# A third weight piece ahead, norms in place, and the query sums moved ahead of the rotations in a two-block fp32 transformer kernel

## The reference

```python
# block 1, per layer (L = 16 + 512)
h = rms_norm(x, norm_g)
z = h @ w_in
q = rms_norm(aq per head, q_norm_g);  k = rms_norm(ak per head, k_norm_g)
q = apply_partial_rope(q, cos, sin);  k = apply_partial_rope(k, cos, sin)
ya = sliding_window_sink_attention(q, k, v, sink) * silu(ag)     # 16 heads of 64, 2 kv heads
mq, mk = silu(causal_depthwise_conv(mq | mk))
log_i = mi + b_i;  log_f = log_sigmoid(mf + b_f)                  # the gates' logs
hm = rms_norm(mlstm_chunkwise(mq, mk, mv, log_i, log_f))
y = concat(ya, hm * sigmoid(mo) * silu(mgate)) @ w_out
x = x + y
```

## Time and profile before

| | |
|---|---|
| median of 3 runs | 3089.79 us (3086.59 to 3089.86) |
| the profiled execution | 3090.76 us, its span 3088.9 us |
| PE busy | 2958.4 us, 96% of the span |
| DVE, ACT, POOL busy | 1617.1, 1264.7, 181.9 us |
| mean granted clock of PE | 0.981 |
| DMA | 250.24 MB, mean 81 GB/s |
| block 1, layers 0 and 1 | about 25 to 637 and 637 to 1236 us |
| block 2, layers 0 and 1 | about 1264 to 2157 and 2186 to 3089 us |

### The profile page before, as it was taken

How to read it: one execution, slowest core, us unless ns; L and a number is a source line. 1 busy time by engine, 2 the same in 40 slices (tenths; PEclk the granted TensorE clock), 3 DMA queues, 4 the chain that set the end, 5 groups by cost and what they waited for, 6 DMA issues and landing times.

```text
span 3088.9 us, 44910 instructions
## 1 busy us (share of the span) xinstructions
PE 2958.4 (96%) x18366; PEld 2582.2 (84%) x18366; DVE 1617.1 (52%) x3255; ACT 1264.7 (41%) x2640; POOL 181.9 (6%) x207
## 2 busy tenths in 40 slices
PE   8899999988999999999999999999999999999998
PEld 6799888987999889888888877887888888877886
DVE  5666645346675453677433564334677433554324
ACT  4455423244554232565424433223566334433222
POOL 2100000010000000100000000000100000000000
PEclk9899999998999999999999999999999999999999
DMA  3111321211113222322233222333322232222222
GB/s 102 55 44 58 105 67 62 86 48 44 57 57 105 67 80 85 113 86 68 82 110 96 69 82 69 96 96 96 113 87 68 82 117 89 81 70 76 95 96 82
DMA packets 99735, 250.24 MB, mean 81 GB/s; under 512 B 8597, under 2 KB 44845, under 8 KB 99274
## 3 DMA queue, kind: packets, MB, share of 16 engines
q1 hardware_dynamic: 99530, 247.37, 25.2%
HBM read 239.60 MB, written 6.50 MB: 80 GB/s over the span
## 4 chain that ended last, share of the span: by engine, by line
PE 81%; DVE 11%; ACT 4%; issue 1%; DMA 1%; POOL 1%; DVEq 0%; POOLq 0%; SPq 0%; ACTq 0%
PE ps L92 78%; PE ps L95 3%; ACT Z L98 2%; DVE cl L101 2%; DVE Z L101 2%; DVE Z L109 1%; DVE ZR L101 1%; DVE Z L119 1%; DMA st<-in_stream_dram 1%; DVE Z L105 1%; DVE stat L122 1%; ACT ch L98 1%; ACT L98 0%; POOL stat L101 0%; DVE sq L109 0%
## 5 line engine op out<-in xcount | busy, mean ns | idle before, releaser
L92 PE MATMUL ps<-hh,ch 128*128 128x264 f32 (+1 forms) x2688 | 824.6, 348 | 54.2 <-DVE cl L101 32.1
L92 PE MATMUL ps<-hl,ch 128*128 128x264 f32 (+1 forms) x2880 | 851.7, 340 | 0.0
L92 PE MATMUL ps<-hh,cl 128*128 128x264 f32 (+1 forms) x2688 | 811.7, 343 | 0.0
L101 DVE TENSOR_TENSOR cl<-st,ch 128x1024 fp32r<-128x1024 f32 (+1 forms) x436 | 495.8, 1152 | 531.3 <-ACT ch L98 531.1
L92 PEld LDWEIGHTS ps<-hh,ch 128*128 128x128 f32 x2688 | 468.4, 192 | 128.7 <-issue 27.4
L98 ACT ACTIVATE ch<-st 128x1024 fp32r<-128x1024 f32 (+1 forms) x436 | 424.8, 990 | 357.0 <-PE ps L92 328.3
L92 PEld LDWEIGHTS ps<-hl,ch 128*128 128x128 f32 x2880 | 500.1, 192 | 59.1
L92 PEld LDWEIGHTS ps<-hh,cl 128*128 128x128 f32 x2688 | 468.4, 191 | 58.9
L98 ACT ACTIVATE Z<-ps 128x512 f32<-128x512 f32 (+7 forms) x510 | 218.9, 438 | 600.3 <-PE ps L92 479.8
L92 PE MATMUL ps<-ZR,ch 128*128 128x264 f32 (+2 forms) x1728 | 426.5, 342 | 5.6 <-DVE cl L101 5.2
L92 PEld LDWEIGHTS ps<-ZR,ch 128*128 128x128 f32 x1728 | 289.1, 191 | 48.8 <-issue 12.9
(11 more groups left out here) (133 smaller groups left out, 3213.6 us busy)
## 6 DMA issues: line engine op xcount, KB each, us to landing
st<-in_stream_dram SPq DMA_DIRECT2D x372, 512.0 KB, 3.6
st<-in_stream_dram SPq DMA_DIRECT2D x64, 256.0 KB, 3.3
Z<-decay_rows SPq DMA_DIRECT2D x8, 904.0 KB, 6.4
Z<-bias_lines SPq DMA_DIRECT2D x16, 448.0 KB, 4.1
ya_spill<-Z SPq DMA_DIRECT2D x8, 512.0 KB, 4.5
Z<-ya_spill SPq DMA_DIRECT2D x2, 2048.0 KB, 7.7
Z<-in_x_dram SPq DMA_DIRECT2D x4, 512.0 KB, 5.6
Z<-in_mem_dram SPq DMA_DIRECT2D x2, 1024.0 KB, 6.1
```

Of the source, the lines that this page charges most:

```text
L92: return Ins(self, self.e and self.e.matmul(o, a, b, start=start, stop=stop, skip_group_check=True))
L101: return Ins(self, self.e and self.e.tensor_tensor(o, a, b, op))
```

## The change

Five things are changed together.

1. One more `weights()` in the lead-in, so that three pieces instead of two stand converted ahead of PE.
2. The norm writes its result `hn` into the memory that `hl` has, and the subtraction hl = hn − hh is made in place by a step `nrml` of its own, one k later. The two `sq` buffers take no part in it.
3. Query tiles 0 and 1 are projected from `RH`/`RL`. DVE multiplies `rstd` in when it reads them, ACT squares the result and then scales it. The norm's parts 5 to 7 come behind tile 0.
4. `chain()` sorts its steps by stage, so that the odd tile's `qsum` comes ahead of the even tile's `rope`, and a `rope` ahead of a `ropeq`.
5. `gra` and the first two `grf` come ahead of attention, beside the first value projections; the other `grf` are two steps earlier, and so is `grt`.

```diff
@@ norms
     def norms(self, nid, *ks):
         for k in ks:
-            self.put("nrm", nid, k, self.nsq())
+            self.put("nrm", nid, k)
+            if k:
+                self.put("nrml", nid, k - 1)
+            if k == 7:
+                self.put("nrml", nid, 7)
@@ chain, qk
-            for t, n, x in todo:
+            for t, n, x in sorted(todo, key=lambda y: y[2]):
...
-            self.proj(("q", l, t), nid, L, u, t % 2)
+            if t < 2:
+                self.projr(("q", l, t), nid, u, t)
+            else:
+                self.proj(("q", l, t), nid, L, u, t % 2)
@@ block1
-        self.norms(nid, 3, 4)
+        self.norms(nid, 3)
         put("gr", l)
-        self.norms(nid, 5, 6, 7)
...
+        self.norms(nid, 4)
         qk(0, u)
+        self.norms(nid, 5, 6, 7)
...
             fill(a - 3)
+            if a == 0:
+                put("gra", l)
+            else:
+                put("grf", l, a - 1)
             chain()
         for s in range(35):
             if s < 32:
                 put("sA", l, s)
-            if s == 0:
-                put("gra", l)
-            if 1 <= s < 9:
-                put("grf", l, s - 1)
-            if s == 5:
+            if 1 <= s < 7:
+                put("grf", l, s + 1)
+            if s == 3:
                 put("grt", l)
@@ lead-in
-        if k in (4, 6):
+        if k in (4, 6, 8):
             m.weights()
@@ ACT, qkev
-                if t == 8:
-                    act.wait_ge(("kz", l))
-                    act.activation(RS[i], QF[i], ACT.Square).then_inc("act_qk", ("qks", l, t))
+                if t in (8, 0, 1):
+                    act.wait_ge(("qz", l, t), ("tk",))
+                    m = act.activation(RS[i], QF[i], ACT.Square)
+                    if t < 8:
+                        m = act.activation(QF[i], QF[i], ACT.Identity, scale=P(f"qg8_{l}"))
+                    m.then_inc("act_qk", ("qks", l, t))
                     return
@@ DVE, nrm and nrml
-                dve.wait_ge(("rstd", nid), *sqw(n))
-                dve.scalar_tensor_tensor(sq[n % 2][:, 0:T], xT[:, k, L - T:L], g, rstd[:, 0:T], ALU.mult,
+                dve.wait_ge(("rstd", nid))
+                if nid:
+                    dve.wait_ge(("full", ("o1", nid - 1, 7) if nid < 3 else ("o2", 0, 7)))
+                dve.scalar_tensor_tensor(hnf[:, k, 0:T], xT[:, k, L - T:L], g, rstd[:, 0:T], ALU.mult,
                                          ALU.mult).then_inc("dve_ns", ("ns", nid, k))
+
+            def nrml(nid, k):
                 if k % 2 == 0:
+                    T = L if nid < 2 else 512
                     dve.wait_ge(("hh", nid, k))
-                    dve.tensor_tensor(hl[:, k, 0:T], sq[n % 2][:, 0:T], hh[:, k, 0:T].bitcast(F32),
-                                      ALU.subtract).then_inc("dve_hl", ("hl", nid, k), ("sqfree", n))
+                    dve.tensor_tensor(hl[:, k, 0:T], hnf[:, k, 0:T], hh[:, k, 0:T].bitcast(F32), ALU.subtract).then_inc(
+                        "dve_hl", ("hl", nid, k))
```

More of the change, by code:

```diff
@@ L362, in norm @@
         for k in range(8):
-            self.put("nrm", nid, k, self.nsq())
+            self.norms(nid, k)
             if k < 7:
@@ L832, in k8 @@
             return ap.rearrange("p (k t) -> p k t", k=8)
-        xT, hh, hl = k8(sb("xT", 8 * L)[:, :]), k8(sb("hh", 8 * L, F32R)[:, :]), k8(sb("hl", 8 * L, F32R)[:, :])
+        xT, hh = k8(sb("xT", 8 * L)[:, :]), k8(sb("hh", 8 * L, F32R)[:, :])
+        with nc.sbuf_tensor("hn", [128, 8 * L], F32) as HN:
+            pass
+        hnf, hl = k8(HN[:, :]), k8(sb("hl", 8 * L, F32R)[:, :])
         ifh, ifl = sb("ifh", 128, F32R), sb("ifl", 128, F32R)
@@ L954, in program @@
         RL = [[zr(o, 528) for o in (11000, 11528, 12056, 12584, 14784, 15312, 15840, 23712)],
-              [zr(o, 528) for o in (0, 528, 1056, 5952, 6480, 8080, 8608, 9136)]]
+              [zr(o, 528) for o in (1056, 1584, 5952, 6480, 8080, 8608, 9136, 23712)]]
         def windows(ap):
@@ L1538, in nrm0, with nrm @@
                 act.activation(rstd[:, 0:T], rstd[:, 0:T], ACT.Exp, scale=-0.5).then_inc("act_norm", ("rstd", nid))
-            def nrm(nid, k, n):
+            def nrm(nid, k):
                 T = L if nid < 2 else 512
                 act.wait_ge(("ns", nid, k))
-                if nid:
-                    act.wait_ge(("full", ("o1", nid - 1, 7) if nid < 3 else ("o2", 0, 7)))
-                act.activation(hh[:, k, 0:T], sq[n % 2][:, 0:T], ACT.Copy).then_inc("act_hh", ("hh", nid, k))
+                act.activation(hh[:, k, 0:T], hnf[:, k, 0:T], ACT.Copy).then_inc("act_hh", ("hh", nid, k))
             def prep():
@@ L1957, in qkev @@
             def qkev(l, t):
-                if t == 8:
-                    key = ("q", l, 8)
+                if t in (8, 0, 1):
+                    key = ("q", l, t)
                     dve.wait_ge(("full", key), ("rstd", l), *bars(("b1", l)))
-                    dve.tensor_tensor(v2(QF[2]), tok(key, L), v2(rstd[:, :]), ALU.mult).then_inc(
-                        "dve_kz", ("free", key), ("kz", l))
+                    dve.tensor_tensor(v2(QF[t % 3]), tok(key, L), v2(rstd[:, :]), ALU.mult).then_inc(
+                        "dve_qz", ("free", key), ("qz", l, t))
             def vev(l, g):
@@ L2543, in final @@
                                              ALU.mult).then_inc("dve_out", ("fo", a))
-            do = dict(w=w, load=load, xt=xt, raw=raw, qkev=qkev, vev=vev, gr=gr, nrm=nrm, prep=prep, rope=rope, qsum=qsum, ropeq=ropeq, qkn=qkn, swap=swap, vtr=vtr, conv=conv, agev=agev,
+            do = dict(w=w, load=load, xt=xt, raw=raw, qkev=qkev, vev=vev, gr=gr, nrm=nrm, nrml=nrml, prep=prep, rope=rope, qsum=qsum, ropeq=ropeq, qkn=qkn, swap=swap, vtr=vtr, conv=conv, agev=agev,
                       m_s=m_s, m_t=m_t, m_o=m_o, sA=sA, sB=sB, grf=grf, grt=grt, ss0=ss0, mA=mA, mB=mB, hsc=hsc,
@@ L2565, in nrm @@
                     pool.wait_ge(("hh", nid, k))
-                    pool.tensor_tensor(hl[:, k, 0:T], sq[n % 2][:, 0:T], hh[:, k, 0:T].bitcast(F32), ALU.subtract).then_inc(
-                        "pool_hl", ("hl", nid, k), ("sqfree", n))
+                    pool.tensor_tensor(hl[:, k, 0:T], hnf[:, k, 0:T], hh[:, k, 0:T].bitcast(F32), ALU.subtract).then_inc(
+                        "pool_hl", ("hl", nid, k))
             def load():
@@ L2587, in mvones @@
             def mvones(l):
-                pool.wait_ge(*bars(("b1", l)), ("full", ("gr", l)))
+                pool.wait_ge(*bars(("b1", l)), ("full", ("q", l, 1)))
                 pool.memset(MV[:, :, :, 256:258], 1.0).then_inc("pool_ones", ("mvones", l))
@@ L2634, in final @@
                 rsqrt(so[:, 8:12], 1024, ("so2",))
-            do = dict(sqa=sqa, dqkev=dqkev, dex=dex, hsc=hsc, memprep=memprep, dnorm=dnorm, final=final, nrm=nrm, load=load, rope=rope, qsum=qsum, vtr=vtr, mvones=mvones, pn=pn, bar=pool.bar)
+            do = dict(sqa=sqa, dqkev=dqkev, dex=dex, hsc=hsc, memprep=memprep, dnorm=dnorm, final=final, nrml=nrml, load=load, rope=rope, qsum=qsum, vtr=vtr, mvones=mvones, pn=pn, bar=pool.bar)
             for kind, *a in steps:
```

5 lines of the change are left out of this document (2 added, 3 removed).

## The result

The changed kernel takes 3167.39 us (median of 4 runs, 3162.19 to 3168.09) beside 3089.82 of before in the same session (3086.59 to 3091.3): a ratio of 1.0257, 95% interval 1.0244 to 1.027. It is 77.6 us slower. The forecast was 3088 us with a range of 3062 to 3104, so the time lies far outside. The profiled execution has a span of 3165.4 us.

The account below looks back on a forecast made before the run. PE is busy nearly throughout, so only about 130 us idle and lowered-clock time could be saved. Terms −5.4 − 11 − 2.4 − 1 + 5.2 + 0 − 4.4 + 17.2 = −1.8 from 3090.8 gave 3089.0, median 3088; range 3062 to 3104.

Parts of the forecast that it names:

- Held conversions: Conversions waiting for the projection in front to end delay ACT's and DVE's work behind them in block 2: +5.2 us.
- two such places in each layer of block 2: PE's 1.43 us wait for ACT and 3.07 us wait for a DVE copy, lengthened by 1.6 and 1.0 us.
- The bound that I gave: Slow end for the held conversions at block 2's two places: 2 × 2 × 2.1 = +8.6 us.
- The rival on held conversions: Block 1 attention's 15 conversion pairs a layer delay softmax work: +16 us, 3104 (3097 to 3112); chance 0.22.
- The rest of the third piece: Fewer `cl` waits: output projection −5.4, kv and first block 2 projection −11, wait at 1528.93 −2.4, small waits −1 us.
- Sums ahead of rotations: DVE waits for POOL at tiles 4 and 6, delaying `QL` and heads 16 and 24: 4 × 4.3 = +17.2 us.
- POOL and DVE block each other: Rival: the norm's sixteen POOL subtractions beside DVE stretch by 0.55 us each, +8.8, 3097 (3090 to 3100); chance 0.08.
- Norm in place and raw tiles: PE's waits for `hl` vanish, but about 6.6 us of waiting returns at the first value tiles: 0 us net.
- Gates' logs: Table loads leave the first heads' exponentials, so the convolved projection starts earlier: −2.2 us a layer, −4.4 in all.
- The clock: PE's clock falls to half behind long gaps; +2 us charged at query tile 2 and for each rotation pair.
- signs "if right": `cl` waits under 30 us, `hl` waits 0, kv waits nearly gone, gap near 4.7 us ahead of heads 16 and 24.
- signs "wrong": No longer gap at heads 16 and 24, many 1 to 2 us gaps in block 1's attention, or value tiles' piece in time.

Follow-up runs that it names:

- e3: The changed kernel with the chain of steps unsorted, sums and rotations in the order of before, third piece still made early: 3119.81 us, ratio 1.0109.
- e7: e4 plus the third converted piece, made right ahead of the next projection instead of right behind the last one: 3061.71 us, ratio 0.9915.
- e2: The kernel before with the third piece converted ahead, made early, and nothing else: 3124.79 us, ratio 1.0121.
- e12: The kernel before with the third piece made late, ahead of the next projection, and nothing else: 3062.68 us, ratio 0.9919.
- e1: The changed kernel with the third piece taken back, so two pieces stand converted ahead, chain still sorted: 3125.04 us, ratio 1.0127.
- e8: e4 with the gates' logs back at their old steps, leaving the norm in place and the two raw query tiles: 3085.27 us, ratio 0.999.
- e11: The kernel before with the gates' logs moved ahead of attention and nothing else: 3081.29 us, ratio 0.9977.
- e6: e4 with a rotation ahead of a tile's last stage (`QL`) in a step's chain, sums keeping their place: 3096.92 us, ratio 1.0031.
- e4: The changed kernel with two pieces ahead and the chain unsorted, leaving in-place norm, raw query tiles and gates' logs: 3082.87 us, ratio 0.9987.
- e5: e4 with the sums first in a step's chain; the odd tile's rotation also came ahead of the even tile's `QL`: 3122.31 us, ratio 1.011.

## Why the prediction was wrong, step by step

**Which step failed.** Two terms of the sum were too small, the held conversions and the sums ahead of the rotations, and together they make nearly the whole error of 79 us.

- *Held conversions, +5.2 us: measured +58 to +62* (e3 against e7, e2 against e12). The failed step is "two such places in each layer of block 2": I priced only the two where PE already waited for ACT or DVE. Of these the one priced at 1.0 us grew by 1.0, and the one priced at 1.6 by less than 0.1. But a hold makes new waits where there was slack under 2.1 us. In e2 the waits for `stat` of L112 (dilated attention) grew from 2.3 to 13.4 us, and in layer 0 of block 2 PE's idle time grew by 16 us and its busy time, for the same matmuls, by 10. The bound that I gave (+8.6) counted only the two places and was no bound. The rival on held conversions had the mechanism and 0.22. Its +16 us for block 1's attention were near what block 1 shows, 14.9; the 43.5 us in block 2 it did not have.
- *The rest of the third piece, −19.8 us (−5.4, −11, −2.4, −1): measured −21 to −25 where the piece is made late.* The size is right partly by luck. −11 were to come at the kv projections, but the waits for `cl` in their two windows fell only from 10.2 to 5.7 us in the changed kernel, and in e7 they did not fall. Most of the gain came ahead of the first convolved projection and of query tile 2, where the gaps of 6.86 and 3.64 us are 2.50 and 0.75 in e12, and for them this term had nothing. With the hold the whole term was −14.6 and is +37 to +42.
- *Sums ahead of rotations, +17.2 us: measured +42 to +48.* The mechanism was right: a DVE wait of 3.2 us at the addition, 3.3 forecast, and gaps of 4.5 us, 4.7 forecast. The size was wrong first because I counted four groups of tiles, "this pair, the same for tiles 6 and 7, two layers". The trace after has the gap ahead of heads 0 and 8 too, eight in all, and the prediction gives no reason for leaving tiles 0 to 3 out. It was wrong also by 1 us a group: 42/8 = 5.3 beside my 4.3. I let the two gaps of 1.21 and 1.19 us become one, but the first stays, so PE's idle time grew by 3.4 us (1.30 + 4.51 − 2.40) where I had 2.3. The clock cost 1.6 us around head 16 in e1 and 3.4 in the changed kernel, where I had 2.
- *POOL and DVE block each other* had 0.08 and was looked for in the norm. It occurs there, for one of POOL's subtractions took 2.32 us in the changed kernel where it took 1.33:

```profile
54.51 2.32 POOL L101 TENSOR_TENSOR hl<-hn,hh 128x528 fp32r<-128x528 f32 x1 [9.79 <-ACT hh L98]
```

But e8, which has the norm in place, shows no loss from it. It occurs as well at the addition (0.71 to 1.74 us) and the pow (1.95 to 2.35 us), as a part of the sorting's cost.

**What held.**

- *Norm in place and raw tiles, 0.* The waits for `hl` are gone and PE waits 6.43 us at the first value tiles, 6.6 forecast. e8, which has this part alone, stands at 0.999 (0.9982 to 0.9999), −3 us by its median. The releaser that the profile names is a `ZR` tile (transposed values and swapped keys), which I had named as what the conversion stands behind.
- *Gates' logs, −4.4: measured −6.4* (e11), with the whole interval on the side of a gain.
- *The clock.* It fell to half behind the new gaps of over 3 us in layer 0 of the changed kernel: behind that of 6.43 us the 10 us from 69 have 0.67, behind that of 4.51 us the 18 us from 218 have 0.81. What such a gap costs is less firm than the +2 that I charged, as e1 and e6 show.

Most of the signs "if right" were there, the waits for `cl` under 30 us and the gap ahead of head 16 among them, and still the time was off by 79 us. One was not: the waits at the kv projections were not nearly gone. And of the signs "wrong", new gaps of 1 to 2 us in block 1's attention, e2 has some (1.17, 1.69 and 1.87 us at 113, 116 and 153 us). The sign that I had not named is ACT's own wait for PE ahead of `ch`, 328 to 782 us. It is a sign and no price, for e7 has 482.7 us of it and is faster.

**What stays open.** The conversions made late gain 21 us on e4, and the waits that the profile puts down to `cl` fell by 8 (29.1 in e4, 20.8 in e7). Those named `issue` fell by 10 more, from 15.6 to 5.3 us. The largest of them in e4 stands ahead of the first convolved projection, where the earlier trace rows has 6.86 us for `cl`, and the conversions stand right in front of it on DVE:

```profile
99.84 2.34 DVE L101 TENSOR_TENSOR cl<-st,ch 128x1024 fp32r<-128x1024 f32 x2
...
101.15 0.78 PE L92 MATMUL ps<-hh,ch 128*128 128x264 f32 x2 [5.46 <-issue]
```

I take it for a wait for `cl` under another name, 5.4 us in each layer; so counted, the waits for `cl` fell by 19 us. What isn't known is why the piece brings nothing at the kv projections when it is made late. Nor did a run separate ACT's hold from DVE's.

The fastest version is e7 (3061.71 us, 0.9915), not told apart from e12 (3062.68 us, 0.9919). e12 is one edit to the kernel before: the third piece, made ahead of the next projection.

## What to carry to other kernels

Work that is moved earlier in an in-order queue brings its waits along. Before moving a prefetch step one place up, look at what frees its buffer and which instruction stands right behind it: here three buffers and three pieces ahead meant that the step could only run at the end of the projection in front, and every eviction stood behind it. The same prefetch, queued behind the evictions, turned +37 us into −21 us, so that the place in the queue was worth 58 us.

Where a step is repeated in groups, count all the groups in the trace before pricing them. And when an experiment sorts or reorders a list that carries over, read the order that came out before reading the time: e5 moved two things at once.

## What the runs showed of the hardware that was not expected

- An addition of 128x528 fp32 on DVE took 1.74 us beside a product of the same size on POOL, 0.71 us alone, in e5. The Trainium skill, Advanced Engine Details and Errata, section Mode Summary, says that VectorE's second SBUF port is shared with GpSimd, and that GpSimd's instructions and VectorE's two-port ones block each other; the prediction's sentence on it leaves the two-port modes out. These rows show such a block for an fp32 addition of two inputs in SBUF, and the addition's 1.03 us more is most of the length of one product (1.30 us).
- POOL's pow of 10 columns took 2.35 us in e5, with DVE's rotation (both inputs in SBUF, 0.70 us) beside it, and 1.95 us in the kernel before, with an operation of 0.68 us beside it that reads one input from PSUM (`ZR<-ps,ZR`, 128x512). So POOL's side stretches as well, but not beside every operation of DVE.
- A single gap of PE doesn't tell whether the clock falls. Behind one of 1.78 us it was 0.50 over the 3 us from 537 in the kernel before, and around one of 2.55 us it stayed 1.00 over 18 us in e6.
